# Encoder layer with routed experts: one group of the next expert's row turns ahead of the second activation turn, weight splits and the silu table moved into ScalarE's waits, four PSUM banks for the first rows

## What is computed

```python
p_group = softmax(t @ w_rg + b_rg); top_p, top_g = top_k(p_group, 1)
sel_logits = (t @ w_re + b_re)[of the chosen group]
top_l, top_e = top_k(sel_logits, 2);  top_w = softmax(top_l)
gate = top_p * top_w   # for 2 of 16 experts per token, 0 elsewhere
for e in range(16):
    a, u = split(t @ w_ei[e], 2)                        # 1024 -> 2 * 512
    y = y + gate[:, e:e+1] * ((silu(a) * u) @ w_eo[e])  # 512 -> 1024
out = layer_norm(ALPHA * x + y)
```

## Time and profile before

| | |
|---|---|
| median of 3 runs | 1349.81 us (1349.29 to 1351.34) |
| profiled execution, its time | 1348.48 us |
| its span | 1346.8 us |
| TensorE busy | 1259.4 us, 94% of the span |
| VectorE, ScalarE, GpSimd busy | 700.6 us, 621.4 us, 352.9 us |
| chain that ended last, by engine | PE 83%, DVE 7%, ACT 4%, issue 3% |
| mean granted TensorE clock | 0.973 |

### The profile page before, as it was taken

The page is one execution under the profiler, slowest core; times in us unless marked ns, Lnnn a source line. Parts: engine busy times, 40 slices in busy tenths (PEclk is TensorE's granted clock), DMA queues, the critical chain, the costliest instruction groups (busy, mean ns, idle before and its releaser), DMA issues.

```text
span 1346.8 us, 19106 instructions
## 1 busy us (share of the span) xinstructions
PE 1259.4 (94%) x7182; PEld 1031.7 (77%) x7183; DVE 700.6 (52%) x890; ACT 621.4 (46%) x844; POOL 352.9 (26%) x306
## 2 busy tenths in 40 slices
PE   5999899999999999999999999589999999989992
PEld 4888867788878888956788878567788788878871
DVE  4233367322476333266522365768755765776456
ACT  4222476432233322276532231667754665775445
POOL 0532000000120332000000020148743746585333
PEclk9999999999999999999999999589999999999996
DMA  6742200023363322200012544469977978898553
GB/s 218 255 145 94 94 1 2 1 94 123 128 235 113 122 94 94 95 32 1 1 63 85 187 151 171 129 226 312 339 263 211 299 230 295 262 354 274 178 180 153
DMA packets 63521, 212.33 MB, mean 158 GB/s; under 512 B 12390, under 2 KB 12902, under 8 KB 62647
## 3 DMA queue, kind: packets, MB, share of 16 engines
q1 hardware_dynamic: 49052, 178.24, 38.4%
q0 software_dynamic: 11808, 24.59, 7.1%
q10 hardware_dynamic: 2592, 8.53, 1.6%
HBM read 199.00 MB, written 34.25 MB: 173 GB/s over the span
## 4 chain that ended last, share of the span: by engine, by line
PE 83%; DVE 7%; ACT 4%; issue 3%; POOL 1%; DMA 1%; ACTq 0%; SPq 0%; DVEq 0%; POOLq 0%
PE banks L736 22%; PE banks L738 22%; PE banks L737 22%; PE banks L902 2%; PE banks L866 2%; PE banks L937 2%; DVE moe_lo L1444 2%; PE banks L1019 2%; PE banks L944 2%; PE banks L877 1%; POOL gated L606 1%; PE banks L770 1%; PE banks L1043 1%; DVE h_full L1842 1%; PE banks L1005 1%
## 5 line engine op out<-in xcount | busy, mean ns | idle before, releaser
L1463 DVE TENSOR_TENSOR wlo<-raw,whi 128x2048 fp32r<-128x2048 f32 (+1 forms) x52 | 116.0, 2231 | 184.3 <-ACT whi L1135 184.3
L1292 ACT ACTIVATE moe_hi<-moe_raw 128x2048 fp32r<-128x2048 f32 x96 | 183.7, 1918 | 48.1 <-PE banks L738 31.9
L1444 DVE TENSOR_TENSOR moe_lo<-moe_raw,moe_hi 128x2048 fp32r<-128x2048 f32 x81 | 183.7, 2290 | 19.5 <-ACT moe_hi L1292 19.4
L736 PE MATMUL banks<-xT,whi 128*128 128x512 f32 x448 | 175.9, 393 | 0.0
L737 PE MATMUL banks<-xT,whi 128*128 128x512 f32 x448 | 175.3, 391 | 0.0
L738 PE MATMUL banks<-xT,wlo 128*128 128x512 f32 x448 | 175.3, 391 | 0.0
L606 POOL TENSOR_TENSOR gated<-gated,kqv 128x512 f32<-128x512 f32 x16 | 25.3, 1598 | 496.7 <-DVE kqv L1605 496.7
L736 PE MATMUL banks<-moe_lo,xeh 128*128 128x512 f32 x368 | 146.6, 398 | 5.4 <-DVE moe_lo L1444 2.3
L736 PE MATMUL banks<-wlo,xT 128*128 128x256 f32 (+1 forms) x448 | 135.4, 302 | 13.0 <-DVE wlo L1463 13.0
L738 PE MATMUL banks<-moe_hi,xel 128*128 128x512 f32 x368 | 144.9, 394 | 0.0
L737 PE MATMUL banks<-moe_hi,xeh 128*128 128x512 f32 x368 | 144.7, 393 | 0.0
(11 more groups left out here) (273 smaller groups left out, 2321.5 us busy)
## 6 DMA issues: line engine op xcount, KB each, us to landing
moe_raw<-in_expert_w SPq DMA_DIRECT2D x192, 512.0 KB
raw<-in_front_w SPq DMA_DIRECT2D x104, 512.0 KB, 4.9
toeplitz_rows<-bias_rows POOLq DMA_DIRECT2D x4, 1152.0 KB, 13.0
kqv<-in_x_turned SPq DMA_DIRECT2D x8, 512.0 KB, 7.6
pt<-in_x SPq DMA_DIRECT2D x2, 2048.0 KB, 10.2
x_rows<-pt ACTq DMA_DIRECT2D x8, 512.0 KB, 2.7
token_sums<-pt ACTq DMA_DIRECT2D x8, 512.0 KB, 3.7
moe_raw<-token_sums SPq DMA_DIRECT2D x8, 512.0 KB, 8.7
```

The source lines that it names most:

```text
L736: mm(dst, left[0], right[1], start=first, stop=False)
L1292: A(moe_hi[m % SPLIT_E], moe_raw[m % RAW_E], ACT.Copy).then_inc(e_hi, 1)
L1444: V.tensor_tensor(moe_lo[m % SPLIT_E], moe_raw[m % RAW_E], moe_hi[m % SPLIT_E].bitcast(F32), ALU.subtract).then_inc(lo_sem(m % ECH), 1)
L1463: V.tensor_tensor(view(lo, shape), view(raw[c % 2], shape), view(hi, shape).bitcast(F32), ALU.subtract).then_inc(w_split, 1)
```

## The change

Six edits:

1. In the tail of the front part ScalarE does `keep_x1` of the last tile ahead of the split of chunk 1.
2. GpSimd's wait for `table_ready` goes from in front of a memset to behind it, directly ahead of the first gather.
3. ScalarE splits chunk 4 right after chunk 3, ahead of the one-hot products, and no longer behind the table.
4. ScalarE loads the silu table (with a dummy silu) ahead of the wait for the table of slots, and no longer behind the splits.
5. The first expert's four groups of rows go to banks 2, 3, 6 and 7, with no wait for `xe_lo` in groups 2 and 3 (`FIRST_BANKS`).
6. In the loop, group 2 of the next rows' turns goes between the first half of `out_part(0, 0)` and `turn_acts(1)`; group 3 stays behind the second half. ScalarE and VectorE copy in the same order: group 2, the second half of the activations, group 3; ScalarE's split of chunk 3 goes behind group 3's copy.

```diff
@@ gpsimd
             pool.wait_ge(const_in, CONSTS)
-            pool.wait_ge(table_ready, 1)
             nc.gpsimd.memset(wait_bearer, 0).then_inc(bearer_ready, 1)
             pool.wait_ge(x1_out, 16 * NT + 1)
+            pool.wait_ge(table_ready, 1)
@@ tensor
-            def turn_rows(b, z, gathers, part):
+            def turn_rows(b, z, gathers, groups, banks=(2, 3, 2, 3)):
                 pe.wait_ge(rows_in[b], gathers * 32)
-                for g in (2 * part, 2 * part + 1):
-                    tb = bank[2 + g % 2]
-                    pe.wait_ge(xe_lo, z * 4 + g + 1)
+                for g in groups:
+                    tb = bank[banks[g]]
+                    if banks[g] < 4:
+                        pe.wait_ge(xe_lo, z * 4 + g + 1)
...
-            turn_rows(0, 0, 1, 0)
-            turn_rows(0, 0, 1, 1)
+            turn_rows(0, 0, 1, range(4), FIRST_BANKS)
...
                     if c == 2:
                         turn_acts(0)
-                        rows_of_next(0)
+                        rows_of_next(0, 1)
...
                 out_part(0, 0, (0,))
+                rows_of_next(2)
                 turn_acts(1)
                 last = out_part(0, 0, (1,))
...
-                rows_of_next(1)
+                rows_of_next(3)
                 pe.wait_ge(h_lo, z * HALVES + 2)
@@ scalar
             e_split(0, 0)
             store_x1(SEQS - 1, 3)
+            keep_x1(SEQS - 1, 3)
             e_split(0, 1)
-            keep_x1(SEQS - 1, 3)
             e_split(0, 2)
...
-            for c in range(EARLY_E, RAW_E):
+            for c in range(EARLY_E, RAW_E + 1):
                 e_split(0, c)
...
+            A(small[:, 59:60], small[:, 58:59], ACT.Silu)
             act.wait_ge(tabled, 2)
...
-            for c in range(RAW_E, SPLIT_E):
+            for c in range(RAW_E + 1, SPLIT_E):
                 e_split(0, c)
-            A(small[:, 59:60], small[:, 58:59], ACT.Silu)
-            rows_hi(0, 0, 0)
-            rows_hi(0, 0, 1)
+            rows_hi(0, 0, range(4), FIRST_BANKS)
...
                 acts_hi(z, 0)
-                rows_hi(1 - b, z + 1, 0)
+                rows_hi(1 - b, z + 1, (0, 1))
                 e_split(pair, b * ECH + 2 + SPLIT_E)
                 gated_half(z, 1)
+                rows_hi(1 - b, z + 1, (2,))
                 acts_hi(z, 1)
+                rows_hi(1 - b, z + 1, (3,))
                 e_split(pair, b * ECH + 3 + SPLIT_E)
-                rows_hi(1 - b, z + 1, 1)
                 e_split(pair, b * ECH + 4 + SPLIT_E)
@@ vector
                 acts_lo(z, 0)
-                rows_lo(1 - b, z + 1, 0)
+                rows_lo(1 - b, z + 1, (0, 1))
                 gated_half(z, 1)
+                rows_lo(1 - b, z + 1, (2,))
                 acts_lo(z, 1)
-                rows_lo(1 - b, z + 1, 1)
+                rows_lo(1 - b, z + 1, (3,))
```

More of the change, by code:

```diff
@@ L186 @@
 POOL_C = 2
+FIRST_BANKS = (2, 3, 6, 7)
 LAST = SEQS * SEQ // P
@@ L1832, in _ @@
                 e_split(0, c)
-            rows_lo(0, 0, 0)
-            rows_lo(0, 0, 1)
+            rows_lo(0, 0, range(4), FIRST_BANKS)
             dve.wait_ge(counted, 1)
```

16 lines of the change are left out of this document (8 added, 8 removed).

## The result

| | before | after |
|---|---|---|
| median, first comparison | 1349.73 us (8 runs, 1346.74 to 1351.34) | 1342.06 us (8 runs, 1339.53 to 1346.49) |
| ratio | | 0.9946, 95% interval 0.9932 to 0.9960 |
| median, second comparison | 1349.9 us (21 runs) | 1343.02 us (8 runs, 1342.03 to 1344.17) |
| ratio | | 0.9957, 0.9943 to 0.9971 |
| profiled execution, its span | 1348.48, 1346.8 us | 1342.55, 1340.9 us |

The change makes the kernel faster by about 7 us, 0.43% to 0.54%. The two spans differ by 5.9 us: 0.30 that the front part happened to end earlier, 4.13 between it and the first expert matmul, and 1.51 in the loop.

The account below looks back on a forecast made before the run. TensorE was taken to bound the loop, and a chain of engine waits the stretch ahead of it. 3.6 us up to the loop + 1.4 - 0.5 - 0.5 in it = 4.0 us, median 1345.8 us, range 1342.3 to 1348.6.

Parts of the forecast that it names:

- rival C: Loop: narrow steps keep their 0.23 us too, as copies follow each other faster; nine times 0.28 more, 1343.3; chance 0.10.
- Edit 1: Last tile's copies: router's product starts 1.5 us earlier, last logits 1.15 earlier; gain 1.15 us, bounds 0.9 and 1.5.
- Edit 2: Wait ahead of the first gather: gain about 0.1 us, rounded to 0.15, bounds 0 and 0.7.
- Edits 3 to 5: First rows' turns: second pair follows the first at once, 1.97 us after its start for 4.25; gain 2.28 us.
- Only together: First rows: the 2.28 us need all three edits; with four banks alone ScalarE would copy group 0 no earlier.
- rival B: First expert matmuls: the turns release the clock, product starts at 2.4 GHz; another 1.8 us, 1344.0; chance 0.12.
- Edit 6, wide steps: Loop: turns cover TensorE's stop; gain 0.23 us in each of six wide steps with next rows, 1.4 us.
- Edit 6, narrow steps: Loop: later h_lo loses about 0.05 us in nine steps (0.5); late chunk-3 split 0.1 each, narrow behind narrow (0.5).
- rival E: Loop: late split of chunk 3 delays loads 1.8 us in five narrow-behind-narrow steps, 9.0 against 4.5 won; 1354.3; chance 0.07.
- Rival D: Loop starts 3.6 us earlier, experts 1 to 3 give half back, loop's 0.4 doesn't come; 1348.0; chance 0.18.
- its own criteria: Wrong if the loop is not within 1 us of 437.4 - 0.4, or first matmul before 880.2 or after 881.7.
- theory 2: Experiments' rival theory: part of the gain is TensorE's varying clock and stops at first expert steps' ends, not the edits' waits.

Follow-up runs that it names:

- the head alone: Edits 1 to 5 with the loop as before, against the kernel before: 1345.32 us for 1349.42, ratio 0.9974.

## Why the prediction was right or wrong

The direction, the order of the edits ahead of the loop and most places of the profile came out; the size was 4.0 where 7 was measured, and the loop, put at 0.4, gave 2 or more. The medians lie below the prices of all five rivals, the lowest of which was C with 1343.3, and C did not happen. So it is partly luck that the outcome lies at the range's edge and not well outside: C and the upper bounds of edits 1 and 2 had widened the range, and neither is what brought the time down. By the steps:

- **Edit 1, forecast 1.15 (0.9 to 1.5).** In the pair of profiles the last logits come 1.20 earlier (851.30 to 850.10), 0.9 without the front part's 0.30. But the table shows that it depends on when TensorE's clock falls in this idle stretch. Where it falls behind the prior product, the last product starts 1.2 to 1.8 us earlier with edit 1 (6.42 to 7.02 for 8.22). Where it falls within it, the tile's turns come later and take 1.95 us, as the changed kernel's second profile shows, and the product starts 0.17 earlier (8.05 for 8.22) or not at all:

```profile
840.44 2.96 PE L771 MATMUL banks<-front_params,gated 128*128 128x20 f32 x16 [0.67 <-ACT gated L1144]
843.24 1.95 PE L760 MATMUL banks<-ident,pt 128*128 128x128 f32 x8
```

  That is the case in three of the eight profiles with edit 1. At the last logits, counted from the end of the front part, it is 0.9 to 1.5 us won in the five profiles of the first kind and 0.1 to 0.3 lost in the three of the second, 0.7 on the average. The forecast took one profile's clock for the kernel's.

- **Edit 2, forecast 0.15.** From the slot table on VectorE to the gather it is 866.80 - 865.58 = 1.22 us, and 868.03 - 866.78 = 1.25 before (the latter start is that of VectorE's row in the profile before): 0.03. GpSimd's own time behind the semaphore hides the memset whole. It was not run alone.

- **Edits 3 to 5, forecast 2.28 and only together.** Together they brought 2.51 us in the run that had them alone and 2.52 in the changed kernel, so the size was right. "Only together" was wrong: 7.79 falls to 5.74 with the banks alone (2.05) and to 6.08 with splits and table alone (1.71). The banks and the two moves on ScalarE remove the same wait from two sides, so they overlap and do not add up. The step that failed is "with four banks alone ScalarE would copy group 0 no earlier than before": true, but what counts is the last copy, and four copies back to back make the delay good.

- **The clock of the first matmuls, rival B (0.12).** I took the loss of the profile before for the changed kernel as well. In five of the eight profiles with edits 3 to 5 together, the product started at full clock, and in none of the six without all three did the clock stay there (with the banks alone it was 0.90 for the first microsecond and 0.53 for the next 3.4). The run of edits 3 to 5 alone is not among the five. In the head's profile, the window of the first matmuls, for the 3.42 us of 8 matmuls shown above:

```profile
880.81:884.20 3.39, 3.39 (x15) 2.82 (x16) 0.00 (x0) 0.24 (x1) 0.48 (x1) 1.00 1.01 400
```

  Fifteen matmuls for eight. So B is not a case that happens or doesn't, but one that comes in a part of the executions: at 1.7 us in five of eight it is about 1.1 us on the average, an estimate from one profile for each run. What I cited from the Trainium skill, page "TensorE: Matmul & The Clock Gate", section "Part 1: The HAM clock gate", that activity releases the throttle, this trace bears out: the clock is 0.56 over the turns (875.87 to 879.22) and 1.00 behind them. The profile after does not show it in time: there the clock is 0.50 over the same turns and for another 4 us of matmuls. What tells the two kinds apart in these eight profiles is when the clock fell in the idle stretch ahead of the turns. In the five it fell between 0.5 us before the turns' start and 0.4 behind it, and was back 3.4 us after the fall, ahead of the product. In the three it fell 0.9 to 2.0 us before the turns' start (at 874.01 in the profile after, for turns at 874.91) and was back only 10.2 us after the fall. What sets the moment of the fall isn't settled here, and the starts of the turns alone (874.90 to 877.39) don't tell the kinds apart.

- **Edit 6, wide steps, forecast 0.23 each.** Measured 0.31 to 0.43, on the average 0.37, 2.2 us for six steps where 1.4 was forecast. In expert 4, from the last matmul of the first half to the first one behind all the turns, it is 994.43 - 991.59 = 2.84 us; before it was 998.11 - 994.92 = 3.19. Of these 0.35, 0.27 are the stall, all of it and not 0.23, and 0.06 come from the turns: three groups of four take 0.44, 0.35 and 0.35 (1.14) where four and eight took 0.41 and 0.79 (1.20).

- **Edit 6, narrow steps, forecast -0.05 each, and -0.1 where narrow follows narrow.** The mechanism is that of the prediction, to a hundredth: the wait for `h_lo` takes the place of the one for `h_full` (2.91 for 2.92 us). But nothing is lost by it, and the late split of chunk 3 costs nothing that shows: steps 3, 11 and 12 sum to 62.5 to 64.6 us in the four profiles with the change's loop and to 61.7 to 65.1 in the seven with the old one. The terms -0.5 and -0.5 of the sum were too dark by 1.0, and rival E, which rests on the same split, has no sign in any profile. Nor does rival C: the narrow steps keep nothing of their 0.23.

- **Rival D.** That experts 1 to 3 give half of the head back does not show in the medians: the head alone won 4.1. In the profile after, though, the loop starts 4.43 us earlier and expert 4 only 3.26, since the first four steps sum to 87.16 us for 85.99; in the head's profile they sum to 84.93. Stops and clock, which differ between executions, make more of these sums than the edits do.

- **Sum.** 0.7 for edits 1 and 2 (a mean over both cases of the clock), 2.5 for 3 to 5, 1.1 for the clock and 2.2 for the loop make 6.5 us, inside both measured intervals (5.4 to 9.2 and 3.9 to 7.7 us). This sum was made after the result, and its 1.1 and 0.7 are means over a few profiles. In the terms of the prediction: edit 6 was too small by 1.8, rival B's share of 1.1 was left out, edits 3 to 5 were 0.2 too small, and edits 1 and 2 were 0.6 too large (0.7 for 1.3). By its own criteria (loop within 1 us of 437.0, first matmul not before 880.2) the profile after stands just outside both, 435.85 and 880.18.

- **What a single profile is worth here.** The spans hold stops and falls of the clock that change from run to run. Over 75 runs of the kernel before, those with a mean granted clock of 0.972 averaged 1350.2 us (17 runs) and those with 0.975 averaged 1347.3 (7 runs). So theory 2 is right in this: the scatter of some 7 us within one kernel goes along with the clock. It does not explain the gain away, since each half of the change moved its own rows by about what the median says, on the same chip as the runs of before. But some of the gain goes along with it: at the same mean clock of 0.975 five runs of the changed kernel averaged 1343.7 us, 3.6 below before's 1347.3, where all runs differ by about 7. The mean clock counts the idle stretches too, which the edits ahead of the loop shorten, so this does not separate a part that is the clock's alone; how much of the 7 us passes through it stays open.

## What to carry to other kernels

When a stop is removed from two sides, ask of each side alone what the last instruction of the chain waits for, not the first: a delay that later work makes up costs nothing. A wait that moves from one place to another in a step that TensorE bounds is worth its length there, and no gain showed from it where the DMA engines are full; so read the steps by kind before multiplying by their number. And before pricing a stretch in which TensorE idles and starts again, look at several profiles, since the clock's fall and rise come at other moments in each, and an edit's worth may hang on them.

## What the hardware showed that I had not expected

- **A branch's place in TensorE's code costs microseconds on the first pass.** With the narrow step in the If's body and the wide one in the Else's, TensorE stopped at the end of steps 0 or 1, or of both, for 0.5 to 4.2 us in each of the eleven profiles, and went on 2.7 to 3.3 us behind the landing of a packet of the instruction queue. With the branches exchanged none of three profiles has such a stop. Not all new code costs one: in the eleven, no such packet comes from 4 us behind the end of step 1 to 2 us ahead of the end of step 13, and the four that come with the code of the last pair (1244.4 to 1292.1 in the changed kernel, both steps wide) have no idle time of 0.2 us or more in TensorE beside them. Why the exchanged order lets the loads come in time is not settled; the packets only show that they come while the step ahead still runs.
- **The clock fell behind such a stop**, in the middle of a product: 0.8 us behind the stop of 2.45 us it went to 0.50, for 3.4 us. Over the fourteen profiles it fell in or behind each of the twelve stops of 2.04 us and more, and behind none of the eight of 1.65 us and less, so a longer stop costs some 1.7 us on top of itself.
- **The removed stop is worth what the next bound leaves of it**: 2.3 us on the median in the changed kernel, 0.5 (not told from nothing) in the kernel before.
- **The table load took 1.28 us and the dummy silu started 0.01 behind it** (869.49 and 870.78 in the profile after), hidden whole in ScalarE's wait.
